# Stick-breaking attention scores: fp32 products replaced by three rounded passes, the keys' low part last

## The reference, cut to what matters

```
q, k, v = jnp.split(h @ w_in, 3, axis=-1)          # 16 heads of 64
q = rms_norm_2(heads(q), q_gain)
k = rms_norm_2(heads(k), k_gain)
for blk in range(S // QB):                         # 4 blocks of 128 queries
    z = einsum('bhtd,bhsd->bhts', q[:, :, t0:kend], k[:, :, :kend]) * scale
    log_stay = where(mask, log_sigmoid(-z), 0.0)
    later = cumsum(log_stay, reverse=True) - log_stay
    weight = where(mask, exp(log_sigmoid(z) + later), 0.0)
    out = einsum('bhts,bhsd->bhtd', weight, v[:, :, :kend])
```

## Time and profile before

| | us |
|---|---|
| median of 3 runs | 1915.99 |
| lowest, highest | 1915.64, 1916.06 |
| the profiled execution's own time | 1915.55 |
| its span in the profile | 1913.8 |

### The profile page before, as it was taken

How to read it: one execution, slowest core, us unless ns; L and a number is a source line. 1 busy time by engine, 2 the same in 40 slices (tenths; PEclk the granted TensorE clock), 3 DMA queues, 4 the chain that set the end, 5 groups by cost and what they waited for, 6 DMA issues and landing times.

```text
span 1913.8 us, 29035 instructions
## 1 busy us (share of the span) xinstructions
PE 1907.8 (100%) x10235; PEld 1617.4 (85%) x10235; DVE 1157.4 (60%) x1685; ACT 886.8 (46%) x1386; POOL 469.4 (25%) x181
## 2 busy tenths in 40 slices
PE   9999999999999999999999999999999999999999
PEld 6777889998888888888889999888777788999887
DVE  5775688866237455464277876423777778787500
ACT  6665544445234434434254444424767554444421
POOL 3323300003423343343420000443322240000243
PEclk9999999999999999999999999999999999999999
DMA  5222233223223232232333222332212132232232
GB/s 177 66 67 78 67 126 117 99 77 106 95 85 106 71 99 82 71 101 74 99 101 131 99 99 76 104 99 78 72 60 66 55 113 97 101 113 93 91 106 89
DMA packets 48889, 177.41 MB, mean 93 GB/s; under 512 B 5552, under 2 KB 6448, under 8 KB 48816
## 3 DMA queue, kind: packets, MB, share of 16 engines
q1 hardware_dynamic: 36864, 137.29, 22.1%
q10 hardware_dynamic: 11952, 39.13, 5.8%
HBM read 174.30 MB, written 2.10 MB: 92 GB/s over the span
## 4 chain that ended last, share of the span: by engine, by line
PE 98%; DVE 1%; ACT 0%; issue 0%; DMA 0%; SPq 0%; DVEq 0%; ACTq 0%
PE B L394 20%; PE B L395 20%; PE B L403 20%; PE B L870 6%; PE B L866 6%; PE B L868 6%; PE B L1224 1%; PE B L415 1%; PE B L1228 1%; PE B L1225 1%; PE B L420 1%; PE B L416 1%; PE B L1405 1%; PE B L1442 1%; PE B L1428 1%; PE B L1052 1%
## 5 line engine op out<-in xcount | busy, mean ns | idle before, releaser
L647 POOL TENSOR_TENSOR WL<-RAW,WH 128x1024 fp32r<-128x1024 f32 (+1 forms) x170 | 458.4, 2699 | 1418.9 <-ACT WH L375 854.8
L375 ACT CAST WH<-RAW 128x1024 fp32r<-128x1024 f32 (+1 forms) x232 | 258.4, 1115 | 444.1 <-PE B L395 358.2
L394 PE MATMUL B<-HH,WH 128*128 128x512 f32 x1064 | 418.9, 394 | 0.3 <-DVE QT L2688 0.3
L395 PE MATMUL B<-HL,WH 128*128 128x512 f32 x1064 | 415.4, 390 | 0.0
L403 PE MATMUL B<-HH,WL 128*128 128x512 f32 x1064 | 265.1, 391 | 0.0
L394 PEld LDWEIGHTS B<-HH,WH 128*128 128x128 f32 x1064 | 200.0, 188 | 42.2 <-issue 1.7
L395 PEld LDWEIGHTS B<-HL,WH 128*128 128x128 f32 x1064 | 200.1, 188 | 39.8
L403 PEld LDWEIGHTS B<-HH,WL 128*128 128x128 f32 x1064 | 196.8, 188 | 40.0 <-POOL WL L647 0.4
L395 PE MATMUL B<-ML,WH 128*128 128x512 f32 x440 | 171.3, 389 | 0.0
L394 PE MATMUL B<-MH,WH 128*128 128x512 f32 x440 | 171.3, 389 | 0.0
L870 PE MATMUL B<-TH,SL 128*128 128x256 f32 x544 | 153.0, 281 | 0.0
(11 more groups left out here) (430 smaller groups left out, 3622.8 us busy)
## 6 DMA issues: line engine op xcount, KB each, us to landing
RAW<-in_w_small SPq DMA_DIRECT2D x186, 512.0 KB, 3.5
RAW<-in_w_large SPq DMA_DIRECT2D x48, 704.0 KB, 4.1
SUMS<-in_w_seven ACTq DMA_DIRECT2D x34, 512.0 KB, 3.6
R<-in_w_seven ACTq DMA_DIRECT2D x17, 512.0 KB, 4.4
HD<-in_w_seven ACTq DMA_DIRECT2D x17, 512.0 KB, 4.4
out_t<-X SPq DMA_DIRECT2D x7, 256.0 KB, 5.2
X<-in_x_t ACTq DMA_DIRECT2D x4, 256.0 KB, 6.3
X<-in_x_t SPq DMA_DIRECT2D x4, 256.0 KB, 6.6
```

What stands on the lines that cost most here:

```text
L375: act.copy(wh, raw).then_inc(s_hi, 1)
L394: pe.matmul(bank, wh[:, c, :], xh[:, k0 + c, :], start=(start and c == 0), stop=False)
L395: mm = pe.matmul(bank, wh[:, c, :], xl[:, k0 + c, :], start=False, stop=False)
L647: pool.tensor_tensor(wl, raw, wh.bitcast(F32), ALU.subtract).then_inc(s_lo, 1)
```

## The change

`QT3` and `KT3` become fp32r tiles, and their two slots now hold the high and the low part of the same pair instead of two pairs' values.

`norm_qk` issues three instructions instead of one: the product written to the high part (which rounds it), the same product written back to `QS` in full fp32, and, after a wait for it, the difference of the two, the low part. Its guard on the earlier scores changes from two stages back to one stage back, since the slots no longer alternate.

`z` issues 24 rounded products instead of eight fp32 ones, in three passes that add up in PSUM: first, in groups of two scores (one for each head), high q by high k and low q by high k; and then, for all eight scores (in stage 0 for four), high q by low k. The first two need k's high part only. Before the last pass stands a wait for k's low part. All increments of `b_z`, by which VectorE learns that a score is complete, are in the last pass. The scores that share bank 4 get a semaphore of their own, `b_open`, so that the two heads do not write to that bank at the same time.

```
                 def z(order):
-                    pe.wait_ge(b_qk, jj * 2 + 2)
+                    pe.wait_ge(b_qk, jj * 2 + 1)
+                    pe.wait_ge(b_hi, jj * 4 + 3)
...
-                    for h, tb, bank, at in order:
+                    def score(h, tb, bank, at, q, k):
                         w = s_width(tb)
                         r = slice(64 * h, 64 * h + 64)
+                        return pe.matmul(B[bank][:, at:at + w], QT3[r, q, P * tb:P * tb + P], KT3[r, k, 0:w],
+                                         start=(at == 0 and q == k), stop=(k == 1), skip_group_check=True)
+                    for n in range(0, len(order), 2):
+                        for q in range(2):
+                            for h, tb, bank, at in order[n:n + 2]:
+                                if q == 0 and h == 1 and bank == 4:
+                                    pe.wait_ge(*((b_open, jj * 2 + 1) if len(order) == 8 else (b_z, jj * 8 + 3)))
+                                mm = score(h, tb, bank, at, q, 0)
+                                if q == 1 and bank == 4:
+                                    mm.then_inc(b_open, 1)
+                    pe.wait_ge(b_qk, jj * 2 + 2)
+                    for h, tb, bank, at in order:
                         if h == 1 and bank == 4:
                             pe.wait_ge(b_z, jj * 8 + 3)
-                        pe.matmul(B[bank][:, at:at + w], QT3[r, jp, P * tb:P * tb + P], KT3[r, jp, 0:w],
-                                  start=True, stop=True).then_inc(b_z, 1)
+                        if h == 0 and bank == 4 and len(order) == 8:
+                            pe.wait_ge(b_open, jj * 2 + 2)
+                        score(h, tb, bank, at, 0, 1).then_inc(b_z, 1)
...
                 def norm_qk(n):
                     dve.wait_ge(b_rq, jj * 2 + n + 1)
                     dve.wait_ge(b_qs, jj * 2 + n + 1)
-                    if not (isinstance(jj, int) and jj < 2):
-                        dve.wait_ge(b_z, jj * 8 - 8)
-                    dve.scalar_tensor_tensor(out=(QT3, KT3)[n][:, jp, :], in0=QS[:, n, :],
-                                             scalar=GAINS[:, G_Q + n:G_Q + n + 1], in1=RQ[:, n, :], op0=ALU.mult,
-                                             op1=ALU.mult).then_inc(b_qk, 1)
+                    if not first:
+                        dve.wait_ge(b_z, jj * 8)
+                    hi, lo = ((QT3, KT3)[n][:, part, :] for part in range(2))
+                    for out in (hi, QS[:, n, :]):
+                        dve.scalar_tensor_tensor(out=out, in0=QS[:, n, :], scalar=GAINS[:, G_Q + n:G_Q + n + 1],
+                                                 in1=RQ[:, n, :], op0=ALU.mult, op1=ALU.mult).then_inc(b_hi, 1)
+                    dve.wait_ge(b_hi, jj * 4 + 2 * n + 2)
+                    dve.tensor_tensor(lo, QS[:, n, :], hi.bitcast(F32), ALU.subtract).then_inc(b_qk, 1)
```

More of the change, by code:

```diff
@@ L248, in build @@
         (M3H, M3L, QT3, KT3, VN3, QS, SQH, SQL, RQ, STAY, BETA, ONES, PT3, HEADMEAN, HEADMEAN32, RAW4, WH4, WL4, LEFT) = scratch([
-            ("M3H", [P, DC, T], F32R), ("M3L", [P, DC, T], F32R), ("QT3", [P, 2, T]), ("KT3", [P, 2, T]),
+            ("M3H", [P, DC, T], F32R), ("M3L", [P, DC, T], F32R), ("QT3", [P, 2, T], F32R), ("KT3", [P, 2, T], F32R),
             ("VN3", [P, 2, TB, P]), ("QS", [P, 2, T]), ("SQH", [P, T], F32R), ("SQL", [P, T], F32R),
@@ L523, in build @@
         b_qs = sem("b_qk_scaled")
+        b_hi = sem("b_qk_high_and_full")
+        b_open = sem("b_first_scores_of_shared_bank")
         b_sq = sem("b_qk_squared")
```

## The result

| | before | changed |
|---|---|---|
| median | 1916.03 us (4 runs) | 1936.9 us (4 runs) |
| lowest, highest | 1915.64, 1916.91 | 1934.57, 1939.68 |
| the profiled execution's own time | 1915.55 | 1936.72 |
| its span | 1913.8 | 1934.9 |
| mean granted TensorE clock | 1.00 | 0.996 |

The ratio is 1.0109 [1.0097, 1.0122]: slower, by 20.9 us between the medians. The prediction said slower, 1930.7, range 1922 to 1936.5; the median is 6.2 us above the forecast and 0.4 above the range.

The account below looks back on a forecast made before the run. TensorE, 98% of the chain that ended last, was taken as the bound. Stages 1 to 7 add 11.9 us and stage 0 2.8, together +14.7: 1930.3, or 1930.7 on the median's scale; range 1922 to 1936.5.

Parts of the forecast that it names:

- the passes: TensorE's 24 rounded score products per stage: 2.45 us against 2.46 before, so they give nothing back by themselves.
- the break at bank 4: Head 1's 256-column score waits for head 0's in bank 4; with such breaks the passes take 1.41 and 1.04 us.
- the ideal sum: TensorE's score products streaming without breaks at bank 4, heads' halves overlapping: 2.1 us per stage.
- the change of tiling: Term at the end of TensorE's scores in the ideal sum: 0.09 us.
- who is stopped, where, and what it costs: Stages 1 to 7: GpSimd's split stops k's low-part subtraction; TensorE loses 1.73 or 1.66 us per stage, 11.9 in all.
- The rival in which only the late stages are lost: VectorE wins where it comes level with GpSimd's split, losing three stages: +7.8 us, 1923.8; chance 0.12.
- the one in which VectorE gets its turn: VectorE's next instruction keeps the port in all stages; only stage 0's +2.8 is left: 1918.8; chance 0.10.
- The rival of halves that do not overlap: Rounded products on TensorE's array halves run in sequence, last pass about 0.5 us longer: +18.7, 1934.7; chance 0.07.
- The granted clock should stay at 1.00, 2.4 GHz, since the gaps are short: TensorE's clock does not fall despite idle gaps of 1.7 us; if it fell, time would be longer than the range.
- stage 0: First stage: later k and a scan stopped by GpSimd's splits cost +2.8 us, bounds 1.6 and 4.
- The start: Stage 0: q's two extra VectorE instructions delay memsets and k's factor, so the scores start +1.36 us later.
- a scan stopped by the splits: Stage 0: VectorE's scan waits until GpSimd's two splits end at 1341.0, moving it and TensorE by 2.7 us.

Follow-up runs that it names:

- the passes alone: Kernel before with TensorE's 24 rounded products in the changed order, all reading high parts only, low parts left out: 1916.0 us, ratio 1.0007.
- the last run: Changed kernel with GpSimd's split that meets k's subtraction waiting until that has ended, operands still in SBUF: 1919.27 us, ratio 1.002.
- the other order: Kernel with PSUM operand and early memsets, plus head 1's 256-column score in bank 4 put last of the eight: 1915.42 us, ratio 0.9995.
- VectorE's part alone: Changed kernel's high, full and low parts on VectorE, but TensorE's eight fp32 scores of before, from full factors: 1929.42 us, ratio 1.0075.

## Why the prediction came out as it did

**Right: the passes.** Reckoned 2.45 us, measured 2.46 in the kernel with the passes alone. The reckoning's single parts were less good: it gave the break at bank 4 about 0.35 per stage, and the order without it returned 0.10; 2.36 us are left where the ideal sum had 2.1, and the sum's 0.09 for the change of tiling stands in no row.

**Right: who is stopped, where, and what it costs.** In stage 1 k's subtraction starts 1.45 us after the high part (1362.18 to 1363.63), as reckoned, GpSimd goes first in all seven stages, and TensorE loses 1.71 to 1.80 per stage at full clock, against 1.73 and 1.66. Five such stages are 8.8 us, and the other two, with the fall taken out, some 3.5: 12.3 against 11.9. The Trainium skill, "SBUF — State Buffer", section "SBUF: two separate sides", calls it an exclusive lock; the run with one operand in PSUM and the run with the split behind agree, with 0.69 us where the stopped one took 2.90. The rival in which only the late stages are lost, and the one in which VectorE gets its turn, are refuted by the same rows. The rival of halves that do not overlap is refuted by the passes alone, although its 1934.7 is nearer to the result: a close time proves no mechanism.

**Wrong: "The granted clock should stay at 1.00, 2.4 GHz, since the gaps are short"**. This is the step that failed. The gaps were as short as predicted, 1.5 us, and the clock fell to 1.2 GHz in stages 3 and 6, 3.4 us each; those periods are 1.4 longer than their neighbours (28.25 against 26.8). That is 2.8 us. In stage 0 it fell for 6.8 us. All four runs of the changed kernel have a mean clock of 0.996. With the gaps filled the kernel takes 1931.5, 0.8 from the forecast and inside its range; 2.1 us of that difference are the transfer below and not the clock. The text did name what a fall would do (a time beyond the range), but gave it neither a chance nor a price. A fall of 3.4 us, the length measured here, can cost at most half of it, 1.7; the rows of before have no fall in the block from which the length could have been read.

**Off in size: stage 0.** Predicted +2.8 (bounds 1.6 and 4), in the profiled executions 1.47 + 2.54 = 4.0. The start, predicted +1.36, came out 0.1 larger. Of the rest, the prediction's mechanism, a scan stopped by the splits, is what happens at full clock: in the last run stage 0 to 1 takes 25.61, +1.84, so 3.3 in all. At half clock the scan comes too late to be stopped and the clock costs instead: 26.31, 0.7 more. The run with the PSUM operand points the same way: its seven executions with a mean clock of 1.00 have a median of 1919.3, the three with 0.998 one of 1920.0, though two of the seven are at 1919.9 and 1920.1 (one more execution has 0.997 and 1924.3).

**Not in the sum: the transfer ahead of the block**, 2.1 us in the profiled execution.

So of the missing 21.2 - 14.7 = 6.5 us, 2.8 are the clock in the loop, 1.2 stage 0, 2.1 the transfer, and 0.4 the size of the stage's loss. The time lies only 0.4 us above the range: without the transfer, which has nothing to do with the change, it would have been inside, with the same wrong step about the clock.

**What stays open.** Why the clock falls in some stages with a gap and not in others. It is not the gap's length alone: the same 1.5 us stood before the fall and before none, in the same kernel and between kernels. Nor is it shown that a gap of this kind is needed. The two kernels without these gaps (the PSUM operand with early memsets, and that with the other order) have 1.00 in all 22 executions, and the changed kernel has 0.996 in four of four. But three executions of the kernel before (1919.37, 1919.6 and 1920.55 us) and two of the passes alone (1919.5 and 1919.86) have a mean clock of 0.999 or 0.998, while the traces of these kernels show no such gap in the block; and of the five executions with the gaps filled one has 0.999. So the gaps make a fall more likely, and what else brings one stays open. Open as well is how often the transfer ahead of the block is late.

## What to carry to other kernels

When an edit adds a VectorE operation with two SBUF operands, look for a GpSimd operation within its time and take it that VectorE loses the longer of the two, and price all that is queued behind it, not its reader alone. An operand in an idle PSUM bank or a wait on the engine that has slack made it free here; a wait put one operation too early moves the meeting to the next one. Where TensorE's stream is dense and an edit puts gaps of 1.5 us into it, give a fall to 1.2 GHz a chance of its own, and count what the slower engine shifts against the others as well.

## What the runs showed of the hardware

- A recorded start 0.01 us behind GpSimd's was enough for VectorE to lose its turn, four times of four. In two of the other runs both were recorded at the same time (1362.09 with VectorE's part alone, 1414.33 with the memsets early), and VectorE lost there too (2.89 and 2.90 us). A start that is level by the rows of before can't be counted as half won.
- A stopped VectorE operation does nothing until GpSimd's has ended: the subtraction ends 0.55 us after it, and the scan, recorded at 3.74, 4.44 and 5.00 us instead of 2.82, ends 2.7 after it each time (1342.12 against 1339.44, 1369.44 against 1366.76, 1348.63 against 1345.96).
- With one operand in PSUM, VectorE's subtraction takes its 0.69 us beside GpSimd's 2.39, and neither is slowed.
- Twenty-four rounded products on alternating halves take 2.46 us, as long as eight fp32 products (sixteen instructions) of the same sizes.
- Gaps of 1.5 us were followed by 3.4 us at 1.2 GHz in two stages of seven of the profiled execution, at a cost of 1.4 us each.
